# Layer ends of a two-block kernel: low parts of five weight chunks moved to GpSimd, half tiles added and turned in another order

## The chip, the core and the metric

One Trainium2 chip, one core. The metric is the device time of one execution in microseconds (us), median of three runs: 1162.67 us before the change (1162.31 to 1165.44). TensorE is called PE in the profile, VectorE DVE, ScalarE ACT, GpSimd POOL, SyncE SP.

## The reference, cut to what matters

The input is one sequence of 256 tokens by 1024 features, float32. Two blocks follow each other. Everything is matrix products of 256 tokens with large weights, and between them norms over the 1024 features:

```python
def first_block(x, ...):
    h = rms_norm(x, norm_mix_pre);  proj = h @ w_in          # attention, conv, gates
    ...
    out = mixed @ w_out
    x = x + rms_norm(out, norm_mix_post)                     # end 1
    h = rms_norm(x, norm_ffn_pre);  u = conv(h @ w_up)
    y = (gelu(u_gate) * u_val) @ w_down
    x = x + rms_norm(y, norm_ffn_post)                       # end 2

def second_block(x, ...):
    x = x + 0.5 * swiglu(rms_norm(x, ffn1_norm), w1, w3, w2) # end 3
    h = rms_norm(x, mix_norm);  p = h @ w_in                 # delta rule, attention
    x = x + (gate_a * y_a + gate_b * y_b) @ w_out            # end 4
    x = x + 0.5 * swiglu(rms_norm(x, ffn2_norm), w1, w3, w2) # end 5
    return rms_norm(x, final_norm)
```

The change is about ends 1 to 4: the stretch in which the last product of a layer is read out, added to x, and x is made the input of the next layer's first product.

## The kernel before, in words

**Chunks.** All weights pass through the core in 172 chunks of 1 MB (128 partitions x 2048 float32), in the order in which the products need them, in a ring of three slots. SP loads chunk n + 3 into `raw` when the low part of chunk n is done. For float32 accuracy with fast products each chunk is split in two: ACT copies it to a rounded high part `w_hi` (L1410), and then `w_lo = raw - w_hi` is computed. Chunks 2 to 25 have their low part made by POOL (L1344), all later ones by DVE (L1695, `split` of the vector program). PE multiplies three times for each product (high x high, low x high, high x low): L2094 to L2096 where the result lies features by tokens (`by_columns`), L2210 to L2212 where it lies tokens by features (`rows_to_tokens`). A by_columns chunk is eight steps k, of six matmuls each. ACT may write `w_hi` of chunk n when PE has used chunk n - 3.

**Numbers used below.** Chunk 43 is the last of end 1 (`A_END` = 44), chunk 76 the last of end 2 (`ffn_at[1]` = 77), chunk 109 the last of end 3 (`B0` = 110), chunk 138 the last of end 4 (`ffn_at[2]` = 139).

**A layer end.** The last chunk leaves four tiles of 128 tokens x 512 features in four PSUM banks, written (t, h) with t the half of the tokens and h the half of the features. Each engine runs its own program in the order written, and they meet in semaphores (`wait_ge`).

- Ends 1 and 2 (`post_norm`): ACT loads the square-root table (L1448), squares each tile with a sum (L1424) and takes the root of each token's mean (L1431). DVE multiplies each tile by the gain (L1744, `gained`), inverts the root (L1747) and adds to x (L1753, `x += gained * 1/root`). Here both inputs of the addition, `gained` and `x`, lie in SBUF; in L1744 one lies in PSUM.
- Ends 3 and 4 (`residual`): DVE adds the bank times a scale to x (L1769); one input lies in PSUM. The tiles are computed in the order (0,0), (1,0), (0,1), (1,1).
- Then PE turns x (L2155, transposes by the identity, eight feature blocks f, four in each half h, two token halves t each), ACT writes the high part `X_hi` of each turned block (L1462), DVE the low part `X_lo` (L1716), and PE starts the next chunk as soon as the first block is there. In ends 1 and 2 all 16 turns stand ahead of the next chunk. In ends 3 and 4 the half h = 0 is turned before the last tile's products, and the half h = 1 inside the next chunk, before its step k = 2 (`turn_late_half`).
- After the eight high parts ACT computes the root for the next layer from x (four squares L1424, then `rcol` L1431) and writes `w_hi` of the third chunk of the next layer; DVE makes diagonals (L1704 to L1709), PE spreads them (L2227, in step k = 3 of the layer's second chunk), ACT copies the result to `rstd` (L1454), DVE reads the first product out (L1807 or L1732) and only then makes `w_lo` of the layer's third chunk.

In a feed-forward layer `Y_hi` (ACT L1544) and `Y_lo = f - Y_hi` (DVE L1835, both inputs in SBUF) feed the down product.

Of the kernel before, what the change touches and what calls it, by code (L numbers as in the profile page):

```python
# [8 lines left out]
F32 = mybir.dt.float32  # L9
# [79 lines left out]
def block_pair(nc, inp, out, scratch, shifted):  # L89

    ctx = ExitStack()
    with ctx:
# [194 lines left out]
                                 lambda i: down_source(2, i))  # L287
        TOTAL = len(chunks)
        BY_POOL = A_GA
        HALF_FIRST = (B0, ffn_at[2])  # L290
        TOKEN_ENDS = (A_END, ffn_at[1], B0, ffn_at[2], TOTAL)
        landed, used = [], [0] * RING
# [1007 lines left out]
        def _(pool):  # L1300
# [61 lines left out]
            for row, part, ap in ((96, 0, inp["rwkv_w_up_2"]), (0, 1, inp["rwkv_a_up_2"]),  # L1362
                                  (0, 0, inp["rwkv_g_up_2"])):
                k = ap.shape[1]
                pool.dma_start(lora_w[row:row + k, part, :], ap[0]).then_inc(S["lora_landed"], 16)

            pool.wait_ge(S["decay_summed"], HT)
            g.tensor_tensor(flat(dec_prev), flat(dec_inv), flat(dec), ALU.subtract).then_inc(  # L1368
                S["sums"], told.one("sums"))
# [6 lines left out]
            for n in range(1, LEVELS + 1):  # L1376
# [14 lines left out]
            pool.wait_ge(S["forget_added"], told.value("forget_added"))  # L1391
            g.tensor_tensor(forget_rows, forget_rows, over(causal[:], NH), ALU.add).then_inc(
                S["forget_added"], told.one("forget_added"))


        @block.scalar
        def _(act):
# [78 lines left out]

            def post_norm(last):

                root_table()
                for t in range(TT):  # L1480
                    root_mean(t, [(bank[4 + 2 * t + h][:, :], *tile_ready(last, t, h)) for h in range(2)],
                              stat[:, 6 + t:7 + t], "post_root")
# [159 lines left out]
            for n in range(A_PA, A_END):  # L1642
                if n == A_PA:
                    for r in PW_ROWS[2:]:
                        silu_rows(r)
                if n < A_WO - 1:
                    split(n + 3)
                if n == A_PA:
                    gate_sigmoids(0)
                if n == A_PA + 1:  # L1650
                    gate_sigmoids(1)
                if n == A_WO - 1 or n == A_WO:
                    for p in (0, 1) if n < A_WO else (2, 3):
                        act.wait_ge(S["mixed"], p + 1)
                        a.activation(X_hi[:, 2 * p:2 * p + 2, :], mixed_a[:, 2 * p:2 * p + 2, :], ACT.Copy).then_inc(
                            S["mixed_hi"], told.one("mixed_hi"))
                if A_WO - 1 <= n < A_END - 1:
                    split(n + 3)
            post_norm(A_END)
# [24 lines left out]
        def _(dve):  # L1684
# [3 lines left out]

            def split(n):

                if n < BY_POOL or n >= TOTAL:
                    return
                slot = n % RING
                dve.wait_ge(S["w_hi"], n + 1)
                v.tensor_tensor(w_lo[slot][:, :], raw[slot][:, :], w_hi[slot][:, :].bitcast(F32),  # L1695
                                ALU.subtract).then_inc(S["w_lo"], told.one("w_lo"))
# [38 lines left out]
            def post_norm(last, next_gain):  # L1735
# [1 line left out]

                e = TOKEN_ENDS.index(last)
                dve.wait_ge(S["gain_landed"], 16 * (e + 1))
                for t in range(TT):  # L1740
                    for h in range(2):
                        c = slice(512 * h, 512 * (h + 1))
                        dve.wait_ge(S["half_squared"], 4 * state["squared"] + 2 * t + h + 1)
                        v.tensor_tensor(gained[:, t, c], bank[4 + 2 * t + h][:, :], token_gain[:, c], ALU.mult).then_inc(  # L1744
                            S["y_gained"], told.one("y_gained"))
                    dve.wait_ge(S["post_root"], 2 * e + t + 1)
                    v.reciprocal(stat[:, 8 + t:9 + t], stat[:, 6 + t:7 + t]).then_inc(  # L1747
                        S["dve_step"], told.one("dve_step"))
                    dve.wait_ge(S["dve_step"], told.value("dve_step"))
                    dve.wait_ge(S["y_gained"], told.value("y_gained"))  # L1750
                    for h in range(2):
                        c = slice(512 * h, 512 * (h + 1))
                        v.scalar_tensor_tensor(out=x[:, t, c], in0=gained[:, t, c], scalar=stat[:, 8 + t:9 + t],  # L1753
                                               in1=x[:, t, c], op0=ALU.mult, op1=ALU.add).then_inc(
                            S["x_updated"], told.one("x_updated"))
                state["squared"] += 2
                for f in range(NT):
                    low_part(f, next_gain, last)
                x_norm()

# [11 lines left out]
            def residual(last, scale, next_gain, base=4):  # L1772

                residual_tile(last, scale, 0, 0, base)
                residual_tile(last, scale, 1, 0, base)
                low_part(0, next_gain, last)
                low_part(1, next_gain, last)
                residual_tile(last, scale, 0, 1, base)
                low_part(2, next_gain, last)
                low_part(3, next_gain, last)  # L1780
                residual_tile(last, scale, 1, 1, base)
                for f in range(4, NT):
                    low_part(f, next_gain, last)
# [294 lines left out]
        def _(pe):  # L2078
# [95 lines left out]
            def turn_late_half():  # L2174


                if state["ends"] in HALF_FIRST:
                    pe.wait_ge(S["x_updated"], 4 * TOKEN_ENDS.index(state["ends"]) + 4)
                    turn_half(1, state["ends"])

            def turn_by_tokens(ends):

# [2 lines left out]
                for h in range(2):  # L2185
                    pe.wait_ge(S["x_updated"], before + h + 1)
                    for f in by_bank(h):
                        turn(f, 0, ends)
                for h in range(2):
                    pe.wait_ge(S["x_updated"], before + 2 + h + 1)  # L2190
                    for f in by_bank(h):
                        turn(f, 1, ends).then_inc(S["x_turned"], told.one("x_turned"))

            def rows_to_tokens(n, slot, both, k0, first, ends=None, base=4):

# [194 lines left out]
```

## Time and profile before

| | |
|---|---|
| median of three runs | 1162.67 us |
| the profiled execution | 1162.08 us, its span 1160.3 us |
| PE, DVE, ACT, POOL busy | 97%, 66%, 48%, 15% of the span |
| matmuls | 9576 |
| mean granted clock of PE | 0.994 of full speed |

The span is the time from the first to the last instruction; the execution's own time is 1.8 us longer. All times in the rows below are counted from the span's start. PE is nearly always busy, so an end matters by the gaps it leaves in PE's row.

### The profile page before, as it was taken

The page shows a single profiled execution, that of the slowest core. Times are in us where ns is not written, and L with a number is a line of the kernel's source. Part 1 is how long each engine was busy: PE and PEld are TensorE (multiplying, and loading weights), DVE is VectorE, ACT ScalarE, POOL GpSimd, SP SyncE. Part 2 cuts the span into 40 slices and gives each one's busy share as a digit, 9 for nine tenths or more (in the row PEclk, how much of TensorE's full clock was granted, in tenths as well). Part 3 has the DMA queues.
Part 4 walks back from the last instruction along what each step waited for, and adds up shares of the span by engine and source line. Part 5 has one row for each costly group of instructions (what it writes and reads, how often), then busy time and mean ns, then how long its engine had stood idle before and what let it go on. Part 6 is the DMA issues. An engine that isn't in the chain of part 4 may idle for free.

```text
span 1160.3 us, 22074 instructions
## 1 busy us (share of the span) xinstructions
PE 1120.8 (97%) x9576; PEld 1060.5 (91%) x9576; DVE 770.0 (66%) x1030; ACT 558.8 (48%) x668; POOL 171.8 (15%) x121
## 2 busy tenths in 40 slices
PE   7999999989899999999999999999999999999997
PEld 6999999989799999889999989999888888999996
DVE  3888976747687767775555567974277676554564
ACT  6333344474765545574343448523334456443343
POOL 4888780000000000000000000123030000000000
PEclk9999999999999999999999999999999999999999
DMA  8586553345356555545556464332143344555651
GB/s 257 190 275 203 179 180 110 110 161 181 124 185 223 175 192 186 181 137 197 175 181 213 153 214 144 113 110 75 42 143 107 129 153 157 205 177 186 212 169 49
DMA packets 146557, 190.00 MB, mean 164 GB/s; under 512 B 7579, under 2 KB 131035, under 8 KB 146351
## 3 DMA queue, kind: packets, MB, share of 16 engines
q1 hardware_dynamic: 145023, 184.28, 47.9%
q0 software_dynamic: 1264, 4.55, 1.1%
q8 instruction: 58, 0.95, 0.3%
q14 instruction: 20, 0.16, 0.0%
q10 hardware_dynamic: 192, 0.05, 0.0%
HBM read 187.79 MB, written 2.65 MB: 164 GB/s over the span
## 4 chain that ended last, share of the span: by engine, by line
PE 87%; DVE 7%; ACT 4%; issue 2%; DMA 0%; ACTq 0%; DVEq 0%
PE bank L2094 21%; PE bank L2095 20%; PE bank L2096 20%; PE bank L2210 6%; PE bank L2211 6%; PE bank L2212 6%; PE bank L579 2%; DVE w_lo L1695 2%; ACT w_hi L1410 1%; PE bank L647 1%; PE bank L2337 1%; DVE bank L1912 1%; PE bank L2155 1%; DVE x L1769 1%; PE bank L554 1%
## 5 line engine op out<-in xcount | busy, mean ns | idle before, releaser
L2094 PE MATMUL bank<-X_hi,w_hi 128*128 128x256 f32 x1840 | 526.3, 286 | 3.2 <-issue 2.6
L2095 PE MATMUL bank<-X_lo,w_hi 128*128 128x256 f32 x1840 | 522.4, 284 | 0.0
L2096 PE MATMUL bank<-X_hi,w_lo 128*128 128x256 f32 x1840 | 522.2, 284 | 0.0
L1410 ACT ACTIVATE w_hi<-w_raw 128x2048 fp32r<-128x2048 f32 x171 | 325.9, 1909 | 159.3 <-PE bank L2096 123.1
L1695 DVE TENSOR_TENSOR w_lo<-w_raw,w_hi 128x2048 fp32r<-128x2048 f32 x146 | 336.6, 2309 | 56.9 <-ACT w_hi L1410 56.6
L2094 PEld LDWEIGHTS bank<-X_hi,w_hi 128*128 128x128 f32 x1840 | 354.5, 193 | 8.8 <-issue 6.8
L2095 PEld LDWEIGHTS bank<-X_lo,w_hi 128*128 128x128 f32 x1840 | 354.7, 193 | 1.2
L2096 PEld LDWEIGHTS bank<-X_hi,w_lo 128*128 128x128 f32 x1840 | 354.6, 193 | 0.0
L1807 DVE TENSOR_TENSOR arena<-bank,rstd 128x512 f32<-128x512 f32 x66 | 45.6, 691 | 184.7 <-PE bank L2096 179.6
L1344 POOL TENSOR_TENSOR w_lo<-w_raw,w_hi 128x2048 fp32r<-128x2048 f32 x24 | 111.3, 4645 | 32.1 <-ACT w_hi L1410 32.0
L2210 PE MATMUL bank<-w_hi,Y_hi 128*128 128x512 f32 x264 | 103.3, 391 | 1.2 <-DVE Y_lo L1835 1.2
L2211 PE MATMUL bank<-w_hi,Y_lo 128*128 128x512 f32 x264 | 103.1, 390 | 0.0
L2212 PE MATMUL bank<-w_lo,Y_hi 128*128 128x512 f32 x264 | 102.7, 389 | 0.0
L1912 DVE SCALAR_TENSOR_TENSOR bank<-arena,par,bank 128x256 f32<-128x256 f32 x232 | 93.2, 483 | 0.6
L1368 POOL TENSOR_TENSOR arena<-arena 128x1024 f32<-128x1024 f32 x1 | 4.4, 4352 | 490.0 <-DVE arena L977 490.0
L2210 PEld LDWEIGHTS bank<-w_hi,Y_hi 128*128 128x128 f32 x264 | 49.7, 188 | 11.1 <-DVE Y_lo L1835 1.6
L2212 PEld LDWEIGHTS bank<-w_lo,Y_hi 128*128 128x128 f32 x264 | 49.6, 188 | 10.5
L2211 PEld LDWEIGHTS bank<-w_hi,Y_lo 128*128 128x128 f32 x264 | 49.7, 188 | 9.1
L1521 ACT ACTIVATE arena<-arena,par 128x256 f32<-128x256 f32 x44 | 24.1, 595 | 69.5 <-DVE arena L1807 69.5
L1530 ACT ACTIVATE arena<-arena 128x512 f32<-128x512 f32 x22 | 13.9, 633 | 84.4 <-DVE arena L1807 84.4
L1732 DVE TENSOR_TENSOR arena<-bank,rstd 128x512 f32<-128x512 f32 x43 | 29.6, 688 | 20.3 <-PE bank L2096 18.0
L1544 ACT ACTIVATE Y_hi<-arena 128x512 fp32r<-128x512 f32 x33 | 20.9, 632 | 44.0 <-DVE arena L1828 44.0
(287 smaller groups left out, 1280.6 us busy)
## 6 DMA issues: line engine op xcount, KB each, us to landing
w_raw<-in_ffn_w_dram SPq DMA_DIRECT2D x66, 1024.0 KB, 5.2
w_raw<-in_w_in_dram SPq DMA_DIRECT2D x53, 1024.0 KB, 5.1
w_raw<-in_w_up_dram SPq DMA_DIRECT2D x22, 1024.0 KB, 5.0
w_raw<-in_w_down_dram SPq DMA_DIRECT2D x11, 1024.0 KB, 4.8
w_raw<-in_w_out_dram SPq DMA_DIRECT2D x8, 1024.0 KB, 4.8
w_raw<-in_conv_pw_w_dram SPq DMA_DIRECT2D x4, 1024.0 KB, 4.9
w_raw<-in_w_attn_out_dram SPq DMA_DIRECT2D x2, 1024.0 KB, 5.0
w_raw<-in_rwkv_proj_dram SPq DMA_DIRECT2D x2, 1024.0 KB, 5.2
```

Of the source, the lines that this page charges most:

```text
L1344: g.tensor_tensor(w_lo[n % RING][:, :], raw[n % RING][:, :], w_hi[n % RING][:, :].bitcast(F32), ALU.subtract).then_inc(S["w_lo_pool"], tol ...
L1410: a.activation(w_hi[slot][:, :], raw[slot][:, :], ACT.Copy).then_inc(S["w_hi"], told.one("w_hi"))
L1695: v.tensor_tensor(w_lo[slot][:, :], raw[slot][:, :], w_hi[slot][:, :].bitcast(F32), ALU.subtract).then_inc(S["w_lo"], told.one("w_lo"))
L1732: v.tensor_tensor(dst, pairs(b), over(rstd[:], 2), ALU.mult).then_inc(S[f"bank{b}_read"], 1)
L1807: v.tensor_tensor(u_t[:, side].rearrange("p (m t) -> p m t", m=2), pairs(2 * (i % 2) + side), over(rstd[:], 2), ALU.mult).then_inc(S[name] ...
L1912: v.scalar_tensor_tensor(out=conv[:, t, :] if k == CONV_W - 1 else part, in0=src, scalar=w, in1=part, op0=ALU.mult, op1=ALU.add).then_inc( ...
L2094: pe.matmul(o, wh, xh, start=start, stop=False, skip_group_check=True)
L2095: pe.matmul(o, wh, xl, start=False, stop=False, skip_group_check=True)
L2096: return pe.matmul(o, wl, xh, start=False, stop=stop, skip_group_check=True)
L2210: pe.matmul(o, yh, wh, start=first and k == 0, stop=False, skip_group_check=True)
L2211: pe.matmul(o, yl, wh, start=False, stop=False, skip_group_check=True)
L2212: mm = pe.matmul(o, yh, wl, start=False, stop=last, skip_group_check=True)
```

## The change

Four things:

1. The low parts of chunks 45, 77, 78, 111 and 140 are made by POOL. The first four stand in POOL's program behind the loads of `lora_w` and ahead of the `decay_summed` subtraction, the fifth is its last instruction. DVE's `split` skips them, and waits for POOL's where the chunk before was POOL's, so that the count stays in order.
2. In end 1 the square-root table is loaded before `w_hi` of chunk 45 instead of behind it.
3. In ends 1 and 2 DVE takes the gains and additions tile by tile in a mixed order, two low parts of x ahead of the last addition; PE turns the last quarter (t = 1, h = 1) inside the next chunk, before its step k = 2.
4. In ends 3 and 4 the addition of tile (0,1) stands ahead of the first low parts of x, not behind the first two.

```diff
+        LOW_BY_POOL = (A_END + 1, ffn_at[0] + 33, ffn_at[0] + 34, ffn_at[1] + 34, ffn_at[2] + 1)
...
+            def low_of(n):
+
+                pool.wait_ge(S["w_hi"], n + 1)
+                pool.wait_ge(S["w_lo"], n - BY_POOL)
+                g.tensor_tensor(w_lo[n % RING][:, :], raw[n % RING][:, :], w_hi[n % RING][:, :].bitcast(F32),
+                                ALU.subtract).then_inc(S["w_lo"], told.one("w_lo"))
+
+            for n in LOW_BY_POOL[:4]:
+                low_of(n)
+
...
+            low_of(LOW_BY_POOL[4])
...
             def post_norm(last):
 
-                root_table()
+                if last != A_END:
+                    root_table()
...
+                if n == A_END - 2:
+                    root_table()
                 if A_WO - 1 <= n < A_END - 1:
                     split(n + 3)
...
             def split(n):
 
-                if n < BY_POOL or n >= TOTAL:
+                if n < BY_POOL or n >= TOTAL or n in LOW_BY_POOL:
                     return
                 slot = n % RING
+                if n - 1 in LOW_BY_POOL:
+                    dve.wait_ge(S["w_lo"], n - BY_POOL)
...
+                gained_tile(0, 0)
+                gained_tile(0, 1)
+                inverse(0)
+                updated_tile(0, 0)
+                gained_tile(1, 0)
+                updated_tile(0, 1)
+                inverse(1)
+                updated_tile(1, 0)
+                gained_tile(1, 1)
+                low_part(0, next_gain, last)
+                low_part(1, next_gain, last)
+                updated_tile(1, 1)
                 state["squared"] += 2
-                for f in range(NT):
+                for f in range(2, NT):
                     low_part(f, next_gain, last)
...
                 residual_tile(last, scale, 0, 0, base)
                 residual_tile(last, scale, 1, 0, base)
-                low_part(0, next_gain, last)
-                low_part(1, next_gain, last)
                 residual_tile(last, scale, 0, 1, base)
-                low_part(2, next_gain, last)
-                low_part(3, next_gain, last)
+                for f in range(4):
+                    low_part(f, next_gain, last)
                 residual_tile(last, scale, 1, 1, base)
...
                 if state["ends"] in HALF_FIRST:
                     pe.wait_ge(S["x_updated"], 4 * TOKEN_ENDS.index(state["ends"]) + 4)
                     turn_half(1, state["ends"])
+                elif state["ends"]:
+                    pe.wait_ge(S["x_updated"], 4 * TOKEN_ENDS.index(state["ends"]) + 4)
+                    for f in by_bank(1):
+                        turn(f, 1, state["ends"]).then_inc(S["x_turned"], told.one("x_turned"))
...
-                for h in range(2):
-                    pe.wait_ge(S["x_updated"], before + 2 + h + 1)
-                    for f in by_bank(h):
-                        turn(f, 1, ends).then_inc(S["x_turned"], told.one("x_turned"))
+                pe.wait_ge(S["x_updated"], before + 3)
+                for f in by_bank(0):
+                    turn(f, 1, ends).then_inc(S["x_turned"], told.one("x_turned"))
```

How the order stands on the engines. On POOL, behind the loads of `lora_w` (called arena here), before:

```order
L1365 DMA arena<-in_rwkv_g_up_dram 96x512
L1368 TENSOR_TENSOR arena<-arena 128x1024 [waits decay_summed]
L1373 DMA bias_by_distance<-arena 8x256 [waits forget]
L1380 TENSOR_TENSOR arena<-arena,levels 128x512 [waits xt_first]
L1380 TENSOR_TENSOR arena<-arena,levels 128x512
```

and now, where `w_lo` is the low part of a chunk, four of them in a row:

```order
L1366 DMA arena<-in_rwkv_g_up_dram 96x512
L1372 TENSOR_TENSOR w_lo<-w_raw,w_hi 128x2048 [waits w_lo,w_hi] x4
L1379 TENSOR_TENSOR arena<-arena 128x1024 [waits decay_summed]
L1384 DMA bias_by_distance<-arena 8x256 [waits forget]
L1391 TENSOR_TENSOR arena<-arena,levels 128x512 [waits xt_first]
```

The fifth stands alone at the program's end. Nothing else on POOL moved.

On DVE at end 2, from the last product of the feed-forward layer on (`arena` stands for f and for `gained`, the number behind `w_lo` is the ring's slot: chunk 77 in slot 2, chunk 78 in slot 0), before:

```order
L1828 TENSOR_TENSOR arena<-arena 128x512 [waits act_gate,conv_val]
L1835 TENSOR_TENSOR Y_lo<-arena,Y_hi 128x512 [waits f_hi,f_ready]
L1695 TENSOR_TENSOR w_lo2<-w_raw2,w_hi2 128x2048 [waits w_hi]
L1695 TENSOR_TENSOR w_lo0<-w_raw0,w_hi0 128x2048 [waits w_hi]
L1744 TENSOR_TENSOR arena<-bank4,arena 128x512 [waits half_squared,gain_landed]
L1744 TENSOR_TENSOR arena<-bank5,arena 128x512 [waits half_squared]
L1747 RECIPROCAL stat<-stat 128x1 [waits post_root]
L1753 SCALAR_TENSOR_TENSOR x<-arena,stat,x 128x512 [waits y_gained,dve_step]
```

and now:

```order
L1859 TENSOR_TENSOR arena<-arena 128x512 [waits act_gate,conv_val]
L1866 TENSOR_TENSOR Y_lo<-arena,Y_hi 128x512 [waits f_hi,f_ready]
L1761 TENSOR_TENSOR arena<-bank4,arena 128x512 [waits half_squared,gain_landed]
L1761 TENSOR_TENSOR arena<-bank5,arena 128x512 [waits half_squared]
L1766 RECIPROCAL stat<-stat 128x1 [waits post_root]
L1773 SCALAR_TENSOR_TENSOR x<-arena,stat,x 128x512 [waits y_gained,dve_step]
L1761 TENSOR_TENSOR arena<-bank6,arena 128x512 [waits half_squared]
L1773 SCALAR_TENSOR_TENSOR x<-arena,stat,x 128x512 [waits y_gained]
L1766 RECIPROCAL stat<-stat 128x1 [waits post_root]
L1773 SCALAR_TENSOR_TENSOR x<-arena,stat,x 128x512 [waits y_gained,dve_step]
```

The two low parts of chunks stand no longer between `Y_lo` and the first gain, and the additions are no longer in pairs; the fourth stands further down, behind two low parts of x. `Y_lo` stands where it stood.

On PE at the same end, behind the last matmul of chunk 76 (x is turned into banks 2 to 5), before:

```order
L2155 MATMUL bank2<-ident,x 128x128
L2155 MATMUL bank3<-ident,x 128x128 x2
L2155 MATMUL bank4<-ident,x 128x128 [waits x_updated]
L2155 MATMUL bank4<-ident,x 128x128
L2155 MATMUL bank5<-ident,x 128x128 x2
L2094 MATMUL bank0<-X_hi,w_hi2 128x256 [waits xg_lo,w_lo]
```

and now:

```order
L2186 MATMUL bank2<-ident,x 128x128
L2186 MATMUL bank3<-ident,x 128x128 x2
L2125 MATMUL bank0<-X_hi,w_hi2 128x256 [waits xg_lo,w_lo]
...
L2127 MATMUL bank0<-X_hi,w_lo2 128x256
L2186 MATMUL bank4<-ident,x 128x128 [waits x_updated]
L2186 MATMUL bank4<-ident,x 128x128
L2186 MATMUL bank5<-ident,x 128x128 x2
```

Twelve matmuls (steps k = 0 and 1) now stand ahead of the last four turns. End 1 has the same two orders.

## Rows read from the trace of the kernel before

**Rows 1.** Page, part 1: busy us (share of the span) xinstructions.
```profile
PE 1120.8 (97%) x9576; PEld 1060.5 (91%) x9576; DVE 770.0 (66%) x1030; ACT 558.8 (48%) x668; POOL 171.8 (15%) x121
```
**Rows 2.** Waits of PE, whole span: us in total, times, longest us.
```profile
PE bank L2155 <- DVE x L1753: 4.9, 4, 1.4
PE bank L2155 <- DVE x L1769: 3.5, 4, 1.5
```
**Rows 3.** Timeline of DVE, end 1: start us, us, engine line op, idle before.
```profile
305.87 1.41 DVE L1753 SCALAR_TENSOR_TENSOR x<-arena,stat,x 128x512 f32<-128x512 f32 x2
```
**Rows 4.** Timeline of ACT, end 1.
```profile
297.25 1.92 ACT L1410 ACTIVATE w_hi<-w_raw 128x2048 fp32r<-128x2048 f32 x1 [3.36 <-PE bank L2212]
299.18 1.28 ACT L1448 ACT_TABLE_LOAD   x1
```
**Rows 5.** Timeline of PE, end 1 to the start of chunk 46.
```profile
306.67 1.32 PE L2155 MATMUL bank<-ident,x 128*128 128x128 f32 x8 [1.40 <-DVE x L1753]
308.29 0.36 PE L2094 MATMUL bank<-X_hi,w_hi 128*128 128x256 f32 x1 [0.30 <-DVE X_lo L1716]
...
320.38 0.39 PE L2094 MATMUL bank<-X_hi,w_hi 128*128 128x256 f32 x1
```
**Rows 6.** Timeline of DVE and ACT behind the high parts of x, end 1.
```profile
310.11 0.87 ACT L1462 ACTIVATE X_hi<-bank,par 128x256 fp32r<-128x256 f32 x2 [0.27 <-DVE X_lo L1716]
318.05 2.28 DVE L1695 TENSOR_TENSOR w_lo<-w_raw,w_hi 128x2048 fp32r<-128x2048 f32 x1
```
**Rows 7.** Timeline of ACT, DVE and PE, end 2.
```profile
488.09 1.90 ACT L1410 ACTIVATE w_hi<-w_raw 128x2048 fp32r<-128x2048 f32 x1
...
490.93 0.69 DVE L1835 TENSOR_TENSOR Y_lo<-arena,Y_hi 128x512 fp32r<-128x512 f32 x1 [0.77 <-ACT Y_hi L1544]
...
491.67 0.50 PE L2210 MATMUL bank<-w_hi,Y_hi 128*128 128x512 f32 x1 [1.22 <-DVE Y_lo L1835]
```
**Rows 8.** POOL beside DVE, us 25 to 40.
```profile
25.71 4.60 POOL L1344 TENSOR_TENSOR w_lo<-w_raw,w_hi 128x2048 fp32r<-128x2048 f32 x1 [0.54 <-ACT w_hi L1410]
27.68 3.18 DVE L1924 TENSOR_TENSOR arena<-arena 128x512 f32<-128x512 f32 x1 [2.25 <-ACT arena L1573]
30.27 9.68 POOL L1344 TENSOR_TENSOR w_lo<-w_raw,w_hi 128x2048 fp32r<-128x2048 f32 x2
```
**Rows 9.** Durations by line, ns min/median/max.
```profile
L1924 DVE TENSOR_TENSOR arena<-arena x4: 692/708/3181, 27.7 to 62.8; 128x512 f32<-128x512 f32 x4
L1732 DVE TENSOR_TENSOR arena<-bank,rstd x20: 691/692/692, 21.6 to 130.5; 128x512 f32<-128x512 f32 x20
```
**Rows 10.** POOL beside DVE, us 725 to 731.
```profile
725.94 4.35 POOL L1368 TENSOR_TENSOR arena<-arena 128x1024 f32<-128x1024 f32 x1 [490.01 <-DVE arena L977]
728.67 2.17 DVE L936 TENSOR_TENSOR arena<-arena 128x512 f32<-128x512 f32 x1
```
**Rows 11.** Windows of PE at a long gap: busy times by engine, then granted clock, DMA share, GB/s.
```profile
242.00:243.00 1.00, 0.00 (x0) 0.00 (x0) 0.50 (x1) 1.00 (x3) 0.00 (x0) 0.89 1.01 418
243.00:244.00 1.00, 0.72 (x3) 0.72 (x4) 0.79 (x2) 0.23 (x1) 0.00 (x0) 0.50 0.99 410
...
246.00:247.00 1.00, 1.00 (x9) 1.00 (x9) 0.29 (x1) 0.76 (x2) 0.00 (x0) 0.91 0.00 0
```
**Rows 12.** That gap in PE's timeline.
```profile
243.28 2.93 PE L2337 MATMUL bank<-arena 128*128 128x128 f32 x12 [3.64 <-ACT arena L1622]
```
**Rows 13.** Timeline of DVE and PE, end 3.
```profile
686.66 2.29 DVE L1695 TENSOR_TENSOR w_lo<-w_raw,w_hi 128x2048 fp32r<-128x2048 f32 x1 [1.98 <-ACT w_hi L1410]
688.31 0.39 PE L2212 MATMUL bank<-w_lo,Y_hi 128*128 128x512 f32 x1
688.87 1.28 DVE L1769 SCALAR_TENSOR_TENSOR x<-bank,x 128x512 f32<-128x512 f32 x2
690.21 0.98 PE L2155 MATMUL bank<-ident,x 128*128 128x128 f32 x7 [1.51 <-DVE x L1769]
...
694.37 0.88 PE L2155 MATMUL bank<-ident,x 128*128 128x128 f32 x6 [0.24 <-DVE x L1769]
```

More of the change, by code:

```diff
@@ L1739, in post_norm, with gained_tile, inverse @@
                 dve.wait_ge(S["gain_landed"], 16 * (e + 1))
-                for t in range(TT):
-                    for h in range(2):
[L1742 to L1745, printed above, removed]
+                def gained_tile(t, h):
+                    c = slice(512 * h, 512 * (h + 1))
+                    dve.wait_ge(S["half_squared"], 4 * state["squared"] + 2 * t + h + 1)
+                    v.tensor_tensor(gained[:, t, c], bank[4 + 2 * t + h][:, :], token_gain[:, c], ALU.mult).then_inc(
+                        S["y_gained"], told.one("y_gained"))
+                def inverse(t):
                     dve.wait_ge(S["post_root"], 2 * e + t + 1)
@@ L1749, in post_norm, with updated_tile @@
                     dve.wait_ge(S["dve_step"], told.value("dve_step"))
[L1750 to L1755, printed above, removed]
+                def updated_tile(t, h):
+                    c = slice(512 * h, 512 * (h + 1))
+                    dve.wait_ge(S["y_gained"], 4 * e + 2 * t + h + 1)
+                    v.scalar_tensor_tensor(out=x[:, t, c], in0=gained[:, t, c], scalar=stat[:, 8 + t:9 + t],
+                                           in1=x[:, t, c], op0=ALU.mult, op1=ALU.add).then_inc(
+                        S["x_updated"], told.one("x_updated"))
+                gained_tile(0, 0)
[10 more added lines that the diff above has]
+                updated_tile(1, 1)
                 state["squared"] += 2
-                for f in range(NT):
+                for f in range(2, NT):
                     low_part(f, next_gain, last)
@@ L2188, in turn_by_tokens @@
                         turn(f, 0, ends)
-                for h in range(2):
-                    pe.wait_ge(S["x_updated"], before + 2 + h + 1)
-                    for f in by_bank(h):
-                        turn(f, 1, ends).then_inc(S["x_turned"], told.one("x_turned"))
+                pe.wait_ge(S["x_updated"], before + 3)
+                for f in by_bank(0):
+                    turn(f, 1, ends).then_inc(S["x_turned"], told.one("x_turned"))
             def rows_to_tokens(n, slot, both, k0, first, ends=None, base=4):
```

## The prediction

> **What bounds the kernel now.** I read the page's busy times first. PE is busy 97% of the span and no other engine is over 66% [rows 1], so only what leaves PE idle, or fills it with other work, moves the time. Then PE's waits over the span: the turns of x wait four times for the additions of ends 1 and 2, 4.9 us in all, and four times for those of ends 3 and 4, 3.5 us in all [rows 2]. That is what the change aims at. Next the timelines of each end, engine beside engine, and last the places where POOL and DVE work side by side, since the change puts POOL beside DVE at all four ends.
>
> One more thing is to be seen behind end 1. PE starts chunk 44 at 308.29 and needs 16 x 0.72 us for chunks 44 and 45 and some 0.5 for the spread, so it comes to chunk 46 at 320.3. The low part of chunk 46 is ready at 318.05 + 2.28 = 320.33 [rows 6] and PE starts it at 320.38 [rows 5]. So behind this end two chains arrive together: PE's own, and the one over ACT's last high part of x (ends at 310.98 [rows 6]), ACT's squares, the root, the spread, DVE's read-out and the low part of chunk 46. A gain must shorten both; a loss in either one counts.
>
> **What POOL does to DVE.** At 25.71 POOL begins a low part of 4.60 us. DVE starts an addition of 512 columns with both inputs in SBUF at 27.68; it is not done before 30.86, after 3.18 us [rows 8], where the same line otherwise takes 0.69 to 0.71 [rows 9]. It ends 0.55 behind POOL's 30.31: it stood still until POOL was done. Later it repeats: POOL's subtraction runs to 730.29, and DVE's two-input operation started at 728.67 ends at 730.84, after 2.17 us [rows 10]. DVE operations with one input in PSUM show none of it: 20 of L1732 between 21.6 and 130.5, most of them beside POOL, took 691 to 692 ns [rows 9]. So DVE operations with both inputs in SBUF wait out a low part on POOL, and the others do not. The Trainium skill has two pages on this. "SBUF — State Buffer", section "Who interferes with whom", says that a DVE instruction with two SBUF inputs and a GpSimd instruction that reads SBUF exclude each other for the whole instruction; by it the sum is the one below, and the rows just named agree. "Advanced Engine Details and Errata", section "VectorE Performance Modes", names only DVE's two-port modes as interfering, which these float32 subtractions would not be in; by it the sum would be the first rival's. The 3.18 us speak against it.
>
> **End 1.** The table load of 1.28 us leaves the path, since ACT stands idle 3.36 us ahead of the high part of chunk 45 [rows 4] and the load fits there. ACT's first square can start at 299.2 instead of 300.6, and its last is bound by the last tile (PE's last matmul of chunk 43 ends at 302.6). DVE has its first two gains done by about 301.6 and would start the first addition at 301.8. But POOL holds chunk 45 from 299.2 (the high part ends at 299.17 [rows 4]) to 303.8, and the addition has both inputs in SBUF. So it starts at 303.7; gain, addition, inverse and third addition follow at 0.6 to 0.75 each, and the third starts at 305.9. Before it started at 305.87 [rows 3]. What the new order and the table would have won, 1.8 us, is eaten by the wait. PE turns the third quarter at about 306.7 as before [rows 5] and starts chunk 44 at 308.35, with 4 turns (0.5 us) still ahead inside it. Those stand behind 12 matmuls, at 309.8; ACT's high part of f = 4 follows 0.5 later and the last one ends at 312.15, not 310.98. So the second chain comes 1.2 us later: +1.2. Without any wait for POOL it would be -0.7 (last high part at 310.2), which is the lower bound.
>
> **End 2.** Here POOL gets chunks 77 and 78. The high part of chunk 77 is done at 489.99 and stands in ACT's program ahead of `Y_hi`, so POOL always starts before `Y_lo` is due. DVE's `Y_lo` = f - `Y_hi` starts at 490.93, has both inputs in SBUF, and PE waits for it already now, 1.22 us, with its first matmul of chunk 76 at 491.67 [rows 7]. With POOL at work from 490.1 to 494.7 it can only start at about 494.6 and end at 495.3: PE starts chunk 76 at 495.35, +3.7. POOL's second one was ready behind the first, but in [rows 8] too the next one was ready and DVE came in between (30.27 and two in 9.68, 0.5 more than 2 x 4.60); it then runs to 499.9. Tiles, squares and roots all move by 3.7, the first addition is due at 500.1 and finds POOL done; from there the mixed order runs undisturbed. Its gain and the later turns nearly cancel in the chain that counts (last high part of x some 0.2 earlier against the rest), so +3.5.
>
> PE's gap before chunk 76 grows to 1.22 + 3.7 = 4.9 us. A gap of 3.64 us [rows 12] is the one place where I see the granted clock fall: 1.00 before, 0.50 (1.2 instead of 2.4 GHz) from just before the work came back at 243.28, and 0.91 in 246 to 247 [rows 11]. That is about 2.8 us of work at half speed, which costs 1.4 us. Gaps of 1.4 us [rows 5] are followed by no such window. I take the 1.4 here: +4.9 for end 2. Bounds: -0.2 if nothing blocks; +9.5 if `Y_lo` must wait for both low parts.
>
> **Ends 3 and 4.** POOL's low part of chunk 111 takes DVE's place of 2.29 us at 686.66. DVE is then free for the additions, which have one input in PSUM, when tiles (0,0) and (1,0) are done (at 686.0 and 687.3, 12 and 6 matmuls of 0.23 us ahead of the one at 688.31), not at 688.87 [rows 13]. They are done by 688.1. PE's first turn follows its 18th matmul at 688.54 instead of 690.21: -1.67. The second wait, 0.24 at 694.37 [rows 13], goes too: the addition of tile (1,1) now stands behind four low parts and ends at about 692.4, when PE comes to step k = 2 at 692.3. ACT's high parts of the second half start 1.9 earlier, so both chains gain: -1.9. POOL is busy until 691.3, and no DVE operation there has two SBUF inputs. End 4 shows the same waits (four waits, 3.5 us, for both ends [rows 2]): -1.9. Bounds for each: 0, if the low parts of x hold the addition back, and -1.9. I take the full value, since all its durations have rows.
>
> **What costs nothing.** Low parts by POOL come 2.3 us later than DVE's, and so do the loads of chunks 48, 80, 81, 114 and 143 behind them; each has over 5 us to its high part. POOL's own later work starts at 725.94 [rows 10], long after 691.3, and its last instruction follows nothing that waits.
>
> **The sum.** 1.2 + 4.9 - 1.9 - 1.9 = +2.3. The profiled execution took 1162.1, so 1164.4 for it; the median shown is 0.6 above it: 1165.0.
>
> **Rivals.**
> - *No blocking at the ends.* POOL's low parts run beside DVE's additions and nothing waits. For it: 20 operations beside POOL keep 692 ns [rows 9]; against it those have a PSUM input, and 3.18 and 2.17 us do not [rows 8, 10]. Then -0.7 - 0.2 - 1.9 - 1.9 = -4.7: 1158.0. Chance 0.14.
> - *`Y_lo` loses twice* (the slower side). If POOL's second low part takes SBUF before the waiting `Y_lo`, PE starts chunk 76 another 4.6 us later: 1169.6. It decides if `Y_lo` would end after 499. [Rows 8] speak against it. Chance 0.07.
> - *Ends 3 and 4 give less*: the addition of tile (1,1) behind four low parts holds the second turn, and the wait of 1.5 comes back in part. With nothing won: 1168.8; with half, 1166.9. Against it: the high part of f = 0 is ready 0.7 behind the turn, so four low parts are done by 691.8. Chance 0.09.
> - *The clock stays up* at end 2: 1163.6. Chance 0.10.
> - My forecast: 0.60, with its own range 1163.3 to 1167.
>
> **How the numbers follow.** What counts as no change is 0.3% or 3.5 us: 1159.2 to 1166.2. Faster holds the first rival: 0.14. Slower holds the second, most of the third (0.07), and the part of my own case above 1166.2, where a further fall of the clock in the sparse turns at either end adds 1.4: 0.15; in all 0.29. Same: 0.57. The range 1157.8 to 1168.0 reaches from the first rival to half of the third.
>
> **What would show it.** In the changed profile: `Y_lo` of chunk 76 at about 4.3 us instead of 0.69 and PE's wait before chunk 76 at 4.9; a window of granted clock 0.5 behind it; the first addition of end 1 at 2.6 us instead of 0.75; PE's wait of 1.51 at ends 3 and 4 gone. If `Y_lo` still takes 0.69, the forecast is wrong by 4.9 + 1.9. If chunk 46 is not what PE waits for behind end 1, my chain there is wrong.

## The result, and the profile after the change

| | before | after |
|---|---|---|
| median of 20 runs on one chip | 1165.38 us (1162.19 to 1166.90) | 1168.05 us (1165.97 to 1169.49) |
| ratio of the times | | 1.0026 [1.0019, 1.0034] |
| profiled execution | 1162.08 us | 1168.08 us |
| its span, mean granted clock | 1160.3 us, 0.994 | 1166.3 us, 0.985 |

The change costs 3.0 us (0.0026 x 1165.4), 2.7 by the two medians. That is under the 0.3% that I called no change, and the median of 1168.05 lies 0.05 us above the top of the range. The executions of the kernel before lie at two levels, 7 of these 20 between 1162.2 and 1162.8 and 13 between 1165.0 and 1166.9. Of the three shown ahead of the prediction two were at the lower one, hence their median of 1162.67; this matters below.

Page, part 1, of the changed kernel. POOL has five instructions more and 23.1 us more work, DVE five fewer [rows 1]:
```profile
PE 1126.8 (97%) x9576; PEld 1066.8 (91%) x9576; DVE 764.1 (66%) x1025; ACT 559.2 (48%) x668; POOL 194.9 (17%) x126
```
PE does the same instructions as before and is busy 6.0 us longer, at a mean granted clock of 0.985 instead of 0.994; the windows further down show where. The waits of PE, which answer to [rows 2] (us in total, times, longest):
```profile
PE bank L2244 <- DVE Y_lo L1866: 4.7, 1, 4.7
PE bank L2186 <- DVE x L1773: 3.5, 4, 1.8
PE bank L2125 <- DVE X_lo L1733: 1.7, 2, 1.0
```
The wait for `Y_lo` of chunk 76 is now the longest one of the kernel. The 3.5 us of waits at ends 3 and 4 are gone: there is no such row any more. Now end 1, in a timeline (start us, us, engine line op, idle before and releaser), which answers to [rows 3 to 6]:
```profile
294.30 1.28 ACT L1460 ACT_TABLE_LOAD   x1
297.64 1.92 ACT L1422 ACTIVATE w_hi<-w_raw 128x2048 fp32r<-128x2048 f32 x1 [1.85 <-PE bank L2246]
299.64 4.58 POOL L1372 TENSOR_TENSOR w_lo<-w_raw,w_hi 128x2048 fp32r<-128x2048 f32 x1 [63.52 <-ACT w_hi L1422]
302.00 2.77 DVE L1773 SCALAR_TENSOR_TENSOR x<-arena,stat,x 128x512 f32<-128x512 f32 x1
304.82 0.66 PE L2186 MATMUL bank<-ident,x 128*128 128x128 f32 x4 [1.84 <-DVE x L1773]
306.08 1.97 PE L2186 MATMUL bank<-ident,x 128*128 128x128 f32 x8 [0.60 <-DVE x L1773]
306.13 0.75 DVE L1773 SCALAR_TENSOR_TENSOR x<-arena,stat,x 128x512 f32<-128x512 f32 x1
320.97 2.28 DVE L1712 TENSOR_TENSOR w_lo<-w_raw,w_hi 128x2048 fp32r<-128x2048 f32 x1
```
The table load lies in ACT's idle time, as forecast. POOL is at work from 299.64 to 304.22. The first addition starts at 302.00, has both inputs in SBUF, and ends at 304.77, 0.55 behind POOL, just as in [rows 8]. The third starts at 306.13 (forecast 305.9, before 305.87). But eight turns take 1.97 us where they took 1.32 [rows 5]: that is the clock. End 2, which answers to [rows 7]:
```profile
493.00 9.46 POOL L1372 TENSOR_TENSOR w_lo<-w_raw,w_hi 128x2048 fp32r<-128x2048 f32 x2 [188.79 <-ACT w_hi L1422]
493.85 4.21 DVE L1866 TENSOR_TENSOR Y_lo<-arena,Y_hi 128x512 fp32r<-128x512 f32 x1 [0.77 <-ACT Y_hi L1557]
498.11 0.80 PE L2244 MATMUL bank<-w_hi,Y_hi 128*128 128x512 f32 x1 [4.73 <-DVE Y_lo L1866]
522.24 2.28 DVE L1712 TENSOR_TENSOR w_lo<-w_raw,w_hi 128x2048 fp32r<-128x2048 f32 x1
```
`Y_lo` takes 4.21 us instead of 0.69, PE waits 4.73 instead of 1.22, and the first matmul behind the gap takes 0.80 instead of 0.50. `Y_lo` came in between POOL's two low parts: 9.46 us for the two is 0.3 more than 2 x 4.58. The windows at both ends (busy us of PE, PEld, DVE, ACT, POOL, then the granted clock, DMA share, GB/s):
```profile
305.00:306.00 1.00, 0.48 (x4) 0.24 (x3) 1.00 (x3) 0.00 (x0) 0.00 (x0) 0.72 0.62 74
310.00:312.00 2.00, 2.00 (x11) 2.00 (x11) 0.53 (x2) 0.00 (x0) 0.00 (x0) 0.50 0.00 0
312.00:314.00 2.00, 2.00 (x18) 2.00 (x17) 1.11 (x3) 1.58 (x4) 0.00 (x0) 0.93 0.00 0
...
497.00:500.00 3.00, 1.89 (x5) 1.52 (x6) 1.06 (x1) 0.07 (x1) 2.86 (x2) 0.50 0.35 91
500.00:503.00 3.00, 3.00 (x9) 2.35 (x8) 0.69 (x1) 0.98 (x3) 2.46 (x1) 0.50 0.73 258
503.00:504.00 1.00, 1.00 (x5) 0.82 (x4) 0.00 (x0) 0.33 (x1) 0.00 (x0) 0.80 0.45 49
...
510.00:512.00 2.00, 1.89 (x9) 1.92 (x10) 1.80 (x4) 0.87 (x2) 0.00 (x0) 0.56 0.04 8
```
At these two ends three stretches stand at 0.50, that is at 1.2 GHz: from 305.4 to about 312.3, from about 496.6 to 503.4, and from about 510.2 to 513.6. In the first profile of before the clock is 1.00 at both ends. Compare 310 to 312 with the same window of before:
```profile
310.00:312.00 2.00, 2.00 (x19) 2.00 (x18) 1.28 (x4) 1.83 (x6) 0.00 (x0) 1.00 0.00 0
```
PE is busy all the time in both, with 19 matmuls before and 11 after. End 3, which answers to [rows 13]:
```profile
696.03 0.69 DVE L1802 SCALAR_TENSOR_TENSOR x<-bank,x 128x512 f32<-128x512 f32 x1 [1.33 <-PE bank L2246]
696.73 4.61 POOL L1372 TENSOR_TENSOR w_lo<-w_raw,w_hi 128x2048 fp32r<-128x2048 f32 x1 [194.26 <-ACT w_hi L1422]
697.39 0.69 DVE L1802 SCALAR_TENSOR_TENSOR x<-bank,x 128x512 f32<-128x512 f32 x1 [0.67 <-PE bank L2246]
698.56 1.04 PE L2186 MATMUL bank<-ident,x 128*128 128x128 f32 x8
...
702.37 1.09 PE L2186 MATMUL bank<-ident,x 128*128 128x128 f32 x8
```
The additions run as soon as their tiles are done, at 0.69 us (the second one beside POOL), and neither group of turns waits.

**Where the time went.** I cut the span at marks that every kernel here has. E1 runs from the pair of low parts on DVE ahead of end 1 (292.12 before) to the start of the low part of chunk 46 (318.05 [rows 6]); E2 from the start of `Y_lo` of chunk 76 (490.93 [rows 7]) to the start of the low part of chunk 79 (512.22); E3 from there to the reciprocal behind end 3 (701.15); E4 from there to the one behind end 4 (972.20). Between E1 and E2 nothing differs (172.88 us in both profiles). In us, before and then the difference to it:

| kernel | E1 | E2 | E3 | E4 | clock at 0.50 at end 1 / end 2 |
|---|---|---|---|---|---|
| before | 25.93 | 21.29 | 188.93 | 271.05 | no / no |
| after | +2.54 | +7.10 | -2.02 | -1.99 | yes / yes, twice |
| forecast | +1.2 | +4.9 | -1.9 | -1.9 | no / yes |

The start of the kernel gives +0.38 (292.50 against 292.12). The sum is +6.0, the difference of the spans.

### The profile page after: what moved, and what is told of

It reads as the page before. It is cut to its first block, busy times and chain, and to the rows that moved or that the text cites. A ratio compares the mean times of both kernels' runs of the same rounds, so it can differ in the third digit from the quotient of the medians.

```text
span 1166.3 us, 22082 instructions
## 1 busy us (share of the span) xinstructions
PE 1126.8 (97%) x9576; PEld 1066.8 (91%) x9576; DVE 764.1 (66%) x1025; ACT 559.2 (48%) x668; POOL 194.9 (17%) x126
## 4 chain that ended last, share of the span: by engine, by line
PE 87%; DVE 6%; ACT 5%; issue 2%; DMA 0%; ACTq 0%; DVEq 0%
PE bank L2125 20%; PE bank L2126 20%; PE bank L2127 20%; PE bank L2244 6%; PE bank L2245 6%; PE bank L2246 6%; PE bank L580 2%; DVE w_lo L1712 1%; ACT w_hi L1422 1%; PE bank L648 1%; ACT sq L1436 1%; PE bank L2186 1%; PE bank L2371 1%; DVE bank L1943 1%; PE bank L555 1%
## 5 line engine op out<-in xcount | busy, mean ns | idle before, releaser
L1712 DVE TENSOR_TENSOR w_lo<-w_raw,w_hi 128x2048 fp32r<-128x2048 f32 x141 | 323.5, 2297 | 51.5 <-ACT w_hi L1422 51.3
L1345 POOL TENSOR_TENSOR w_lo<-w_raw,w_hi 128x2048 fp32r<-128x2048 f32 x24 | 111.3, 4648 | 32.3 <-ACT w_hi L1422 32.1
L1372 POOL TENSOR_TENSOR w_lo<-w_raw,w_hi 128x2048 fp32r<-128x2048 f32 x5 | 23.1, 4623 | 550.4 <-ACT w_hi L1422 550.3
```

Of the source, the lines that this page charges most:

```text
L1345: g.tensor_tensor(w_lo[n % RING][:, :], raw[n % RING][:, :], w_hi[n % RING][:, :].bitcast(F32), ALU.subtract).then_inc(S["w_lo_pool"], tol ...
```

## The experiments

Ten more runs were made, in three groups, each with its own executions of the kernel before: e1 to e4 (median 1165.45 of 35), e5 to e8 (1165.66 of 23), e9 and e10 (1165.67 of 20). The changed kernel did not run again in them, so a difference to it is one between two ratios to before; by their intervals it is uncertain by some 1.5 us either way. Two theories stood against each other for the end that costs most: the time is lost because POOL holds SBUF against one operation of DVE, or it is lost with the order and the turns that were rewritten. A third question was what the clock takes of it. The same four differences for every kernel, from its profile, beside its measured ratio:

| kernel | ratio to before | E1 | E2 | E3 | E4 | clock fell at end 1 / 2 |
|---|---|---|---|---|---|---|
| e1_45_111_140 | 0.9975 [0.9964, 0.9987] | +0.87 | +0.39 | -2.02 | -1.93 | no / no |
| e2_111_140 | 0.9965 [0.9949, 0.9980] | +1.20 | +0.40 | -2.01 | -1.98 | yes / no |
| e3_order_only | 0.9989 [0.9977, 1.0001] | +0.04 | +0.39 | -0.29 | -0.22 | no / no |
| e4_before_77_78 | 1.0027 [1.0016, 1.0038] | +1.50 | +3.98 | +0.01 | -1.41 | yes / yes |
| e5_gain_in_psum | 0.9999 [0.9989, 1.0008] | -0.95 | +7.05 | -2.01 | -1.92 | no / yes, twice |
| e6_psum_and_wait | 0.9949 [0.9934, 0.9965] | -0.94 | -0.30 | -2.00 | -1.94 | no / no |
| e7_filled_gap | 1.0007 [0.9994, 1.0019] | +2.59 | +3.33 | -2.02 | -1.91 | yes / no |
| e8_before_again | one profile, 1165.46 us | +1.51 | +1.02 | +0.02 | +0.07 | yes / yes |
| e9_before_111_140 | 0.9968 [0.9954, 0.9981] | 0.00 | +1.50 | -1.72 | -1.66 | no / yes |
| e10_wait_only | 1.0006 [0.9993, 1.0018] | +0.85 | +4.10 | -2.02 | -1.94 | no / yes |

**e1_45_111_140: chunks 77 and 78 back to DVE.**
```
-        LOW_BY_POOL = (A_END + 1, ffn_at[0] + 33, ffn_at[0] + 34, ffn_at[1] + 34, ffn_at[2] + 1)
+        LOW_BY_POOL = (A_END + 1, ffn_at[1] + 34, ffn_at[2] + 1)
```


> The changed kernel with the low parts of chunks 77 and 78 back on DVE; 45, 111 and 140 stay on POOL. My theory (POOL's low part shuts out DVE's operations with both inputs in SBUF, and the gap it makes also costs clock): end 2 loses nothing any more, Y_lo of chunk 76 takes 0.69 us, end 1 still costs 1.2 to 2.6, ends 3 and 4 give 2.0 each; 1 to 3 us faster than before and 5 to 8 faster than the changed kernel. Rival (the new order of turns and additions is what costs, not POOL): end 2 stays as slow as in the changed kernel, within 1 us of it.

Measured 1162.31 us, 2.9 faster than before, as expected. Timeline of its DVE:
```profile
301.69 2.78 DVE L1773 SCALAR_TENSOR_TENSOR x<-arena,stat,x 128x512 f32<-128x512 f32 x1
...
491.86 0.69 DVE L1866 TENSOR_TENSOR Y_lo<-arena,Y_hi 128x512 fp32r<-128x512 f32 x1 [0.77 <-ACT Y_hi L1557]
```
With POOL away from end 2, `Y_lo` is back at 0.69 us; with POOL still at end 1, the first addition there still takes 2.78. The two chunks cost 0.0051 of the time, 5.9 us, by the ratios of after and of this kernel. That is more than the whole loss of 3.0: without them the kernel is faster than before.

**e2_111_140: chunk 45 back as well** (`LOW_BY_POOL = (ffn_at[1] + 34, ffn_at[2] + 1)`).

> As the one before, and chunk 45 back on DVE too: POOL makes only 111 and 140. My theory: end 1 costs about nothing, so 3.5 to 4.5 us faster than before, about 2.5 faster than with chunk 45 on POOL. Rival (the new order costs at end 1): no difference to the kernel with 45 on POOL, the third addition of end 1 no earlier.

1160.58 us, 4.1 faster than before, in the range expected; against e1 it is 1.2 us faster, less than expected, and the two intervals overlap. In the profiles E1 is even longer here than in e1, because this execution lost the clock at end 1 and that one did not (e3, with the same end 1 and no fall, has +0.04).

**e3_order_only: no low part on POOL** (`LOW_BY_POOL = ()`); the order of the additions and turns and the early table load stay.

> The changed kernel with all five low parts on DVE: the new order of additions and turns and the earlier table load alone. My theory: at ends 3 and 4 the additions again wait behind DVE's own low part (first at 688.9 on before's clock) and PE's wait of 1.5 us is back, so within 1 us of before. Rival (the earlier third addition is what shortens ends 3 and 4): 3 to 4 us faster than before, as fast as with 111 and 140 on POOL.

1162.87 us, ratio 0.9989: 1.3 us faster, where within 1 was expected, and the interval just holds 1. PE's waits for additions and for the first low part of x:
```profile
PE bank L2185 <- DVE x L1772: 3.3, 6, 1.0
PE bank L2185 <- DVE x L1801: 3.0, 2, 1.5
PE bank L2124 <- DVE X_lo L1732: 1.9, 2, 1.0
```
The first row is ends 1 and 2: 4.9 us of waits [rows 2] became 3.3, yet E1 and E2 did not get shorter (+0.04 and +0.39). The last row shows where most of it went: with another gain ahead of it on DVE, the first low part of x is now waited for by 1.0 us at each of these ends, where it was 0.3 [rows 5]. The middle row is ends 3 and 4: the two waits of 1.5 stay, and the two short ones (0.24 [rows 13]) are gone. So the new order alone is worth 0.2 to 0.3 at each of ends 3 and 4, and the 1.5 are POOL's doing.

**e4_before_77_78: the kernel before, with chunks 77 and 78 by POOL and nothing else of the change** (`LOW_BY_POOL = (ffn_at[0] + 33, ffn_at[0] + 34)`, the function `low_of`, its calls and DVE's skip).

> The kernel before with one thing changed: the low parts of chunks 77 and 78 by POOL, nothing else. My theory: Y_lo of chunk 76 takes about 4.2 us, PE waits 4.7 us ahead of chunk 76 and its clock falls to half behind it; 5 to 8 us slower than before. Rival (POOL and DVE do not shut each other out): DVE's first gain is earlier, 0 to 1 us faster than before.

1167.9 us, 3.1 slower. The mechanism is there with the old order too. PE's wait, and a window behind it:
```profile
PE bank L2223 <- DVE Y_lo L1848: 4.7, 1, 4.7
```
```profile
498.00:501.00 3.00, 2.85 (x7) 2.27 (x8) 0.09 (x1) 0.00 (x0) 3.00 (x1) 0.50 0.73 211
```
The size was expected at 5 to 8: a miss. Its span is 5.5 us longer than that of the first profile of before, but E2 has only +3.98 of it, since the clock was back soon after 501. The rest stands where this kernel does what the kernel before does: 1.45 lie ahead of E1 (e5 has 1.44 there), 1.50 are a clock fall at end 1, where this kernel is the kernel before, and -1.41 in E4 is a fall that the first profile has at 867 to 871 and this one has not.

**e5_gain_in_psum: the gained tile stays in its PSUM bank**, so that the addition of ends 1 and 2 has one SBUF input.
```
-  v.tensor_tensor(gained[:, t, c], bank[4 + 2 * t + h][:, :], token_gain[:, c], ALU.mult)
+  v.tensor_tensor(bank[4 + 2 * t + h][:, :], bank[4 + 2 * t + h][:, :], token_gain[:, c], ALU.mult)
-  v.scalar_tensor_tensor(out=x[:, t, c], in0=gained[:, t, c], scalar=stat[:, 8 + t:9 + t], ...)
+  v.scalar_tensor_tensor(out=x[:, t, c], in0=bank[4 + 2 * t + h][:, :], scalar=stat[:, 8 + t:9 + t], ...)
```


> The changed kernel, all five low parts on POOL, but in ends 1 and 2 the gained tile is written back into its PSUM bank, so that the addition to x has one input in PSUM. My theory (only operations with both inputs in SBUF are shut out): the first addition of end 1 takes about 0.7 us instead of 2.8, end 1 gives 0.5 to 1 against before; Y_lo of chunk 76 still takes 4.2 us. 2 to 4 us faster than the changed kernel. Rival (any DVE operation waits, or it is the order of the semaphores): no change against the changed kernel.

1165.4 us, 0.0027 or 3.1 us under after, as expected. POOL and the first addition of end 1:
```profile
300.70 4.59 POOL L1372 TENSOR_TENSOR w_lo<-w_raw,w_hi 128x2048 fp32r<-128x2048 f32 x1 [63.49 <-ACT w_hi L1422]
303.07 0.75 DVE L1773 SCALAR_TENSOR_TENSOR x<-bank,stat,x 128x512 f32<-128x512 f32 x1
```
The same addition, beside the same work of POOL, takes 0.75 us in place of 2.77. Only the place of the gained tile differs. E1 falls to -0.95. `Y_lo`, which still reads SBUF twice, takes 4.21 as in after, and E2 keeps its +7.05.

**e6_psum_and_wait: e5, and POOL begins chunk 77 only when `Y_lo` is done.**
```
+                if n == ffn_at[1]:
+                    pool.wait_ge(S["f_lo"], FPAIRS)
                 pool.wait_ge(S["w_hi"], n + 1)
```


> As the one before, and POOL starts the low part of chunk 77 only when Y_lo of chunk 76 is done. My theory: Y_lo takes 0.69 us again, PE's wait of 4.7 us is 1.2 again, no addition waits for POOL; all four ends give: 4.5 to 6.5 us faster than before. Rival (POOL now ends chunk 78 too late, at about 501 on before's clock, and its successors' loads and high parts are late): no faster than the kernel with only 111 and 140 on POOL.

1158.43 us (1156.68 to 1160.40), ratio 0.9949: 5.9 us faster than before, as expected, and 9 faster than after. Its timeline at end 2:
```profile
490.45 0.69 DVE L1868 TENSOR_TENSOR Y_lo<-arena,Y_hi 128x512 fp32r<-128x512 f32 x1 [0.77 <-ACT Y_hi L1559]
491.23 9.31 POOL L1374 TENSOR_TENSOR w_lo<-w_raw,w_hi 128x2048 fp32r<-128x2048 f32 x2 [186.90 <-DVE Y_lo L1868]
496.13 0.75 DVE L1775 SCALAR_TENSOR_TENSOR x<-bank,stat,x 128x512 f32<-128x512 f32 x1
```
`Y_lo` is done before POOL starts, and the additions run at 0.75 us beside it. No part of the change was dropped. That it is also faster than e2, which leaves POOL only chunks 111 and 140, is not shown by the times: 1.9 us by the ratios, with intervals that overlap. The profiles speak for it: E1 -0.94 and E2 -0.30 here, against +0.04 and +0.39 in e3, which like this one shows no fall.

**e7_filled_gap: after, with 19 matmuls into an unused bank ahead of PE's wait for `Y_lo`.** They add work and change no output.
```
+                if k == 0:
+                    split_ready(b0 + 32)
+                    for _ in range(19):
+                        pe.matmul(bank[2][:, :], X_hi[:, 0, 0:P], w_hi[(b0 + 32) % RING][:, 0:512], start=True, stop=True)
                 pe.wait_ge(S["f_lo"], before + FPAIRS)
```


> The changed kernel with 19 more matmuls of 512 columns (0.23 us each, 4.3 us, into an unused bank) on PE while it waits for Y_lo of chunk 76; the wait itself stays. They hold the clock, and nothing else is changed. My theory (the gap also costs clock): no window of granted clock 0.5 behind the gap, 1.4 to 3 us faster than the changed kernel, though PE does more. Rival (the wait alone is the loss of end 2): no change, or up to 0.3 us slower.

1165.02 us, 0.0019 or 2.2 us under after, in the range expected; the intervals of the two ratios just touch. PE at the gap, then a window that was at 0.50 in after:
```profile
493.22 4.47 PE L2290 MATMUL bank<-w_hi,X_hi 128*128 128x512 f32 x19
498.22 0.50 PE L2244 MATMUL bank<-w_hi,Y_hi 128*128 128x512 f32 x1 [0.53 <-DVE Y_lo L1866]
```
```profile
498.00:502.00 4.00, 3.78 (x17) 3.14 (x18) 0.85 (x2) 1.65 (x5) 4.00 (x1) 1.00 0.80 251
```
PE comes to chunk 76 at 498.22, even 0.11 later than in after, and yet E2 is 3.77 us shorter (+3.33 against +7.10), without a window at 0.50. These 3.77 are the clock's. What is left, 3.33, is the block, together with what the new order does at this end (+0.39 in e1 to e3, where nothing is blocked). In the three profiles with the gap left empty (after, e4, e5) the clock fell at it each time.

**e8_before_again: the kernel before, unchanged, one more profile.**

> The kernel before once more, for one more profile: its own runs lie at two levels, 1162.6 and 1165.6. If these are falls of PE's clock at gaps where it sometimes holds, this profile shows the same waits as the first and differs in the windows of granted clock alone.

1165.46 us, span 1163.5, against 1162.08 and 1160.3 in the first profile. The waits are the same (4.8 and 3.5 where [rows 2] have 4.9 and 3.5), but:
```profile
310.00:312.00 2.00, 2.00 (x12) 2.00 (x10) 1.79 (x5) 1.73 (x6) 0.00 (x0) 0.50 0.00 0
...
504.00:506.00 2.00, 2.00 (x11) 1.80 (x10) 1.79 (x5) 1.75 (x5) 0.00 (x0) 0.50 0.04 8
```
The clock fell at the turns of both ends, with the same program and the same gaps. It took 1.51 and 1.02 us. That is 2.5 of the 3.2 us between the two spans.

**e9_before_111_140: the kernel before, with only chunks 111 and 140 by POOL.**

> The kernel before with one thing changed: the low parts of chunks 111 and 140 by POOL; the third addition stays behind two low parts of x. My theory (DVE's own low part is what the additions of ends 3 and 4 wait for): the first addition starts at 686.1 instead of 688.9, PE's waits of 1.5 us go, a wait of up to 0.6 stays ahead of the second turn; 1.3 to 1.7 us a layer end, 2.6 to 3.4 us faster than before. Rival (the gain needs the third addition ahead of the low parts): under 1 us faster.

1161.33 us, ratio 0.9968, 3.7 us faster, 0.3 more than the range expected; E3 and E4 have -1.72 and -1.66, 3.4 together. End 3:
```profile
688.31 0.69 DVE L1783 SCALAR_TENSOR_TENSOR x<-bank,x 128x512 f32<-128x512 f32 x1 [1.33 <-PE bank L2226]
690.83 0.38 PE L2169 MATMUL bank<-ident,x 128*128 128x128 f32 x2
694.93 1.09 PE L2169 MATMUL bank<-ident,x 128*128 128x128 f32 x8 [0.26 <-DVE x L1783]
```
The first turns do not wait although the third addition stands where it stood. The wait of 0.26 at the second turns is what the new order takes away.

**e10_wait_only: after, and POOL waits for `Y_lo` as in e6, with the gained tile in SBUF.**

> The changed kernel, and POOL starts the low part of chunk 77 only when Y_lo of chunk 76 is done; the gained tiles stay in SBUF. My theory: Y_lo takes 0.69 us, but now the additions of end 2 meet the two low parts (4.6 us each, from 491.7 on before's clock): the first one ends only at about 496.3 or, if it comes just behind the change of hands, 500.9, and costs up to 4 us; 1 to 4 us faster than the changed kernel and 2 to 5 slower than the same with the gained tiles in PSUM. Rival (only Y_lo matters): as fast as the kernel with the gained tiles in PSUM and the wait.

1165.58 us, 2.3 us under after, in the range expected, and 6.6 over e6, where 2 to 5 were expected. End 2:
```profile
493.36 9.28 POOL L1374 TENSOR_TENSOR w_lo<-w_raw,w_hi 128x2048 fp32r<-128x2048 f32 x2 [188.71 <-DVE Y_lo L1868]
498.26 4.93 DVE L1775 SCALAR_TENSOR_TENSOR x<-arena,stat,x 128x512 f32<-128x512 f32 x1
```
The block moved from `Y_lo` to the first addition, which came just after POOL's second low part had begun and waited out nearly all of it. PE stood 4.2 us for it, and the clock fell there too. Either mend alone gives 2.3 to 3.1 us against after, and both together 9: PSUM alone leaves `Y_lo` to be held, the wait alone leaves the first additions of both ends.

## Why the prediction was wrong, point by point

I forecast a loss of 2.3 us against the execution profiled; the ratio gives 3.0. The mechanism, its place and its sign were right. The time was still outside the range: the median of after lies 3.05 us above the forecast of 1165.0, and two things made that, a term that was mis-sized, the clock, and the base to which the loss was added.

**The step that failed** is the clock. At end 2 the prediction said: "That is about 2.8 us of work at half speed, which costs 1.4 us." It cost 3.77 (after against e7). PE resumed at 498.11 and the clock stayed at 0.50 until 503.4, some 5.3 us of work, which is 2.6 us lost by the same halving; I had taken the length of the fall from [rows 11], where it ended 2.8 us behind the gap. Then it fell a second time, from about 510.2 to 513.6, behind the turns, for the other 1.1. At end 1 the prediction gave no clock term: "Gaps of 1.4 us [rows 5] are followed by no such window." The clock fell at 305.4, behind a gap of 1.84 and ahead of one of 0.60, and it took 1.7 us (+2.54 in after and +2.59 in e7 with the fall, +0.87 and +0.85 in e1 and e10 without). e8 shows that even the 1.4 us gaps of before can be followed by one. I had read "no fall in one profile" as "no fall". And the 3.64 us gap was not "the one place": the very profile that I read has two more falls, behind waits of 1.96 and 2.44 us (timeline of PE, then windows):
```profile
867.56 0.80 PE L708 MATMUL bank<-arena 64*128 64x128 f32 x4 [1.96 <-DVE arena L1119]
894.13 0.44 PE L757 MATMUL bank<-arena 128*64 128x128 f32 x4 [2.44 <-ACT arena L889]
868.00:870.00 2.00, 2.00 (x12) 1.78 (x11) 1.03 (x3) 0.43 (x3) 0.00 (x0) 0.50 0.03 11
896.00:898.00 2.00, 2.00 (x11) 2.00 (x11) 1.62 (x6) 1.08 (x6) 0.00 (x0) 0.50 0.81 229
```
With these rows a wait of 1.8 us at end 1 could not be called safe. I had put a further fall into the upper part of my own case, with 1.4 us; there were two further ones and the first was longer, 4.1 us more than the term in the sum (1.7 at end 1 and 2.4 at end 2).

**The base.** The median of the three executions shown was 1162.67, and the profiled one took 1162.08, without a fall at ends 1 and 2. Over 20 and 35 runs the median is 1165.4, which is where e8 lies, with its two falls. So I added the loss to a time 2.7 us too low. Of the 3.05 us by which the forecast was short, 2.7 are this base and 0.35 the loss itself: the falls cost the changed kernel 4.1 us more than I gave them, but a typical execution of before has 2.5 us of falls at the same two ends (e8), which the one profiled did not have. So the base and the falls are one error seen twice: a profile without falls at ends 1 and 2 as the base, and as the model of what follows. It is also why the ratio gives 3.0 us and the two profiles 6.0. The slowest of the three executions shown, 1165.44, had been a sign of it.

Two sums of the prediction do not come out, though neither changes the forecast: half of the third rival is 1166.9, not the 1168.0 of the range's top, and the difference between my case and no blocking is 7.0 us, not 4.9 + 1.9.

The other steps:
- *POOL holds DVE's operations with two SBUF inputs.* Right. `Y_lo` 4.21 us (forecast about 4.3), first addition 2.77 (forecast 2.6), additions with a PSUM input 0.69 beside POOL; e5 turns the block off by moving one input. PE's wait 4.73 (forecast 4.9). The Trainium skill, page "SBUF — State Buffer", section "Who interferes with whom", states this, and says that the order of issue decides who stands: the 4.93 us of e10, where POOL had started first, agree. The Trainium skill's page "Advanced Engine Details and Errata", section "VectorE Performance Modes", names only DVE's two-port modes as interfering. The 4.21 and 2.77 us show a block of operations that give no sign of such a mode: the addition takes 0.75 us undisturbed both with two inputs in SBUF (the third one of end 1) and with one in PSUM (e5).
- *End 1, +1.2.* The part of it without the clock is +0.87. The chain was right: in e1, without a fall, the last high part of x ends at 312.14 (forecast 312.15), and in after PE starts chunk 46 at 323.31, just behind its low part (320.97 + 2.28). The bound of -0.7 for no blocking came out at -0.95 (e5).
- *End 2, 3.5 for the block.* 3.33 in e7, with the new order in both, right.
- *Ends 3 and 4, -1.9 each.* -2.02 and -1.99, right, and rightly put down to POOL for the larger part: 1.7 of it (e9), and 0.2 to 0.3 for the third addition's new place (e3).
- *What costs nothing*: outside the four stretches after differs from before only by 0.38 us at the start, so nothing of POOL's later work or the later loads entered; the low parts on POOL at ends 3 and 4 bring the same in every kernel that has them.

The rivals: *no blocking* fell with the 4.21 us. `Y_lo` *loses twice* did not happen; it came in between POOL's two. *Ends 3 and 4 give less* fell. *The clock stays up* fell in all three profiles with the gap.

What stays open: why the clock falls at the sparse turns in one execution and not in the next (e8 against the first profile of the same program; after and e7 against e1 and e10, which have the same end 1). The runs show that it does, not what decides it. So the differences of single profiles at ends 1 and 2 hold only beside the column that tells whether the clock fell.

## What to carry to other kernels

Before work goes to POOL, list DVE's operations with both inputs in SBUF that will fall beside it, and give each what is left of POOL's instruction when it comes (3.5, 2.0 and 4.2 us here); an input left in PSUM, or a wait that lets DVE's critical operation go first, takes the price away, and it must be done for every such operation, since mending one shows the next. Price a longer PE wait by the wait plus the clock behind it, which was as large here as the block itself. Take more than one profile of the kernel before as the base where PE's work is sparse.

## What the runs showed of the hardware that I had not expected

- A fall of the granted clock to 0.50 came and went between executions of one program, at gaps of at most 1.4 us (e8), and at one of 1.84 us between kernels with the same end 1. It took 1.0 to 1.7 us each time.
- Filling PE's wait with 19 matmuls whose result nobody reads (4.47 us) made the kernel 2.2 us faster than leaving it idle, with the wait's end 0.11 us later.
- A waiting operation of DVE gets SBUF ahead of POOL's next one although that is ready: at end 2 of after, `Y_lo` ended at 498.06 and POOL's pair took 0.3 us more than its two parts. In e10 an operation that came late stood for 4.93 us, its own 0.75 and 4.2 of POOL's 4.6.
